# Sparse attention: one shift and one reciprocal for the four row tiles of a head, with waits for the whole head

## The reference, cut to what matters

```python
def attend_block(args):
    ...
    score = jnp.where(causal[None], score, -jnp.inf)
    _, idx = lax.top_k(score, topk)
    valid = idx <= t_pos[None, :, None]
    k_sel = gather(k, idx)
    v_sel = gather(v, idx)
    logits = jnp.einsum('bthd,btjd->bthj', q_b, k_sel).astype(jnp.float32) * ATTN_SCALE
    logits = jnp.where(valid[:, :, None, :], logits, -jnp.inf)
    probs = jax.nn.softmax(logits, axis=-1).astype(v.dtype)
    return jnp.einsum('bthj,btjd->bthd', probs, v_sel)
...
return (o * jax.nn.silu(z)) @ w_out
```

## Time and profile before

| | |
|---|---|
| median of 3 runs | 1798.1 us (1792.12 to 1801.71) |
| span of the profiled execution | 1793.1 us; its own time is not listed apart, and the median is 5.0 us above the span |
| TensorE busy | 1615.7 us (90%) |
| VectorE busy | 723.9 us (40%) |
| ScalarE busy | 520.4 us (29%) |
| GpSimd busy | 593.7 us (33%) |
| mean granted TensorE clock | 0.912 of full speed |
| masks, exponentials and scalings of the 16 heads | from 770.8 to 953.3 us of the span |

### The profile page before, as it was taken

The page is one execution under the profiler, slowest core; times in us unless marked ns, Lnnn a source line. Parts: engine busy times, 40 slices in busy tenths (PEclk is TensorE's granted clock), DMA queues, the critical chain, the costliest instruction groups (busy, mean ns, idle before and its releaser), DMA issues. The chain is left out here.

```text
span 1793.1 us, 23133 instructions
## 1 busy us (share of the span) xinstructions
PE 1615.7 (90%) x9729; PEld 1347.6 (75%) x9729; DVE 723.9 (40%) x1479; ACT 520.4 (29%) x842; POOL 593.7 (33%) x247
## 2 busy tenths in 40 slices
PE   6998999999989978988998989679999877959899
PEld 6896876999978755856667988677887643548889
DVE  4022430231252646967662161402301455587331
ACT  2443224332122232233442122432221234311211
POOL 5333421333332464426532433132442260500213
PEclk9998999999999988999999999889999776569769
DMA  4222310324223211311113222222332000000103
GB/s 148 92 71 71 94 47 1 95 95 177 71 71 107 79 63 47 94 48 47 42 43 133 80 94 88 98 66 75 94 95 71 1 1 1 0 30 1 63 20 102
DMA packets 116913, 121.58 MB, mean 68 GB/s; under 512 B 14799, under 2 KB 111033, under 8 KB 116554
## 3 DMA queue, kind: packets, MB, share of 16 engines
q1 hardware_dynamic: 109232, 111.90, 19.8%
q10 hardware_dynamic: 7578, 8.21, 1.4%
HBM read 113.80 MB, written 6.29 MB: 67 GB/s over the span
## 5 line engine op out<-in xcount | busy, mean ns | idle before, releaser
L175 POOL TENSOR_TENSOR w_low<-w_ring,w_high 128x2048 fp32r<-128x2048 f32 (+2 forms) x95 | 422.4, 4448 | 927.3 <-ACT w_high L166 927.2
L191 PE MATMUL ps<-w_high,xT_high 128*128 128x256 f32 (+1 forms) x1056 | 306.7, 290 | 32.7 <-ACT heads L1753 11.8
L191 PE MATMUL ps<-w_low,xT_high 128*128 128x256 f32 (+1 forms) x1056 | 301.6, 286 | 0.0
L191 PE MATMUL ps<-w_high,xT_low 128*128 128x256 f32 (+1 forms) x1056 | 301.5, 285 | 0.0
L166 ACT ACTIVATE w_high<-w_ring 128x2048 fp32r<-128x2048 f32 (+2 forms) x95 | 174.1, 1834 | 372.2 <-PE ps L191 359.5
L191 PE MATMUL ps<-xT_high,w_high 128*128 128x512 f32 (+3 forms) x624 | 255.0, 409 | 8.7 <-DVE mix_a L724 7.7
L191 PE MATMUL ps<-xT_low,w_high 128*128 128x512 f32 (+3 forms) x624 | 250.9, 402 | 0.0
L191 PE MATMUL ps<-xT_high,w_low 128*128 128x512 f32 (+3 forms) x624 | 250.6, 402 | 0.0
L191 PEld LDWEIGHTS ps<-w_high,xT_high 128*128 128x128 f32 x1056 | 205.7, 195 | 38.8 <-DVE xT_low L826 12.1
L191 PEld LDWEIGHTS ps<-w_low,xT_high 128*128 128x128 f32 x1056 | 205.6, 195 | 1.3 <-issue 1.2
L191 PEld LDWEIGHTS ps<-w_high,xT_low 128*128 128x128 f32 x1056 | 205.2, 194 | 0.0
(11 more groups left out here) (499 smaller groups left out, 2422.5 us busy)
## 6 DMA issues: line engine op xcount, KB each, us to landing
w_ring<-in_gla_w_in_dram SPq DMA_DIRECT2D x24, 1024.0 KB, 5.4
w_ring<-in_dsa_w_in_dram SPq DMA_DIRECT2D x19, 1024.0 KB, 5.2
w_ring<-in_w_in_dram SPq DMA_DIRECT2D x18, 1024.0 KB, 5.2
w_ring<-in_gla_w_out_dram SPq DMA_DIRECT2D x8, 1024.0 KB, 5.2
w_ring<-in_ple_gate_w_dram SPq DMA_DIRECT2D x8, 1024.0 KB, 5.0
w_ring<-in_dsa_w_out_dram SPq DMA_DIRECT2D x8, 1024.0 KB, 5.0
w_ring<-in_w_out_dram SPq DMA_DIRECT2D x8, 640.0 KB, 4.2
x_scratch<-x SPq DMA_DIRECT2D x4, 1024.0 KB, 6.8
```

The costliest lines, as they stand in the source:

```text
L175: self.nc.gpsimd.tensor_tensor(self.w_low[:, i % RING, 0:k, 0:cols], self.w_ring[:, n % RING, 0:k, 0:cols], self.w_high[:, i % RING, 0:k, ...
L191: return self.nc.tensor.matmul(out, lhs, rhs, start=first, stop=last, skip_group_check=not check)
```

## The change

The four shifts of a head become one operation on four columns behind the fourth mask, and the four reciprocals one operation behind the fourth exponential. ScalarE waits once a head, for that shift; VectorE waits for all four exponentials before the reciprocal, and for the reciprocal before the first scaling. The semaphores `peak_shift` and `inv_total` count heads instead of row tiles. Nothing else is changed.

```diff
@@ exps(h), ScalarE
-                        act.wait_ge(sem["peak_shift"], past["peak_shift"] + m + 1)
+                        if j == 0:
+                            act.wait_ge(sem["peak_shift"], past["peak_shift"] + h + 1)
@@ mask(h), VectorE
-                        dve.wait_ge(sem["masked"], past["masked"] + m + 1)
-                        nc.vector.tensor_scalar(shift[:, i:i + 1], peak[:, i:i + 1], -ATTN_SCALE, None, ALU.mult).then_inc(sem["peak_shift"], add("peak_shift", 1))
+                    heads = slice(h % 2 * NT, (h % 2 + 1) * NT)
+                    dve.wait_ge(sem["masked"], past["masked"] + NT * (h + 1))
+                    nc.vector.tensor_scalar(shift[:, heads], peak[:, heads], -ATTN_SCALE, None, ALU.mult).then_inc(sem["peak_shift"], add("peak_shift", 1))
@@ normalise(h), VectorE
+                    heads = slice(h % 2 * NT, (h % 2 + 1) * NT)
+                    dve.wait_ge(sem["exps"], past["exps"] + NT * (h + 1))
+                    nc.vector.reciprocal(inv[:, heads], total[:, heads]).then_inc(sem["inv_total"], add("inv_total", 1))
+                    dve.wait_ge(sem["inv_total"], past["inv_total"] + h + 1)
                     for j in range(NT):
                         m = NT * h + j
                         i = m % (2 * NT)
-                        dve.wait_ge(sem["exps"], past["exps"] + m + 1)
-                        nc.vector.reciprocal(inv[:, i:i + 1], total[:, i:i + 1]).then_inc(sem["inv_total"], add("inv_total", 1))
-                    for j in range(NT):
-                        m = NT * h + j
-                        i = m % (2 * NT)
-                        dve.wait_ge(sem["inv_total"], past["inv_total"] + m + 1)
                         row = prob[:, h % 2, j, 0:(j + 1) * P]
                         nc.vector.tensor_scalar(row, row, inv[:, i:i + 1], None, ALU.mult).then_inc(sem["prob_ready"], add("prob_ready", 1))
```

## The result

| | before | after |
|---|---|---|
| median, 4 runs each | 1795.1 us (1788.4 to 1801.7) | 1848.6 us (1842.4 to 1854.4) |
| ratio | | 1.0292 [1.0262, 1.0322] |
| span of the profiled execution | 1793.1 us | 1849.6 us (own time 1851.4) |
| TensorE, VectorE busy | 1615.7, 723.9 us | 1633.3, 741.9 us |
| mean granted TensorE clock | 0.912 | 0.904 |

The change makes the kernel 53 us slower, 2.9%. VectorE has six operations less in each head and is busy for 18 us more.

A forecast was written before the change was run, and what follows sets the result against it. TensorE was taken to bound iterations with a projection, with no slack in the chain through VectorE's copy of `probT`; the terms summed to 55.9 us on the 1798.1 median, giving 1854 us, range 1842 to 1866.

The forecast's parts named there:

- term 6: Iterations 12 and 13, already bound by the copy's chain: exponentials 1.5 us later, third scaling caught, 0.35; together 3.7 us.
- Terms 2 and 3: Head loop: `gT_high` 1.0 to 1.5 us later; third scaling falls 0.01 to 0.08 us behind `gT_low` instead of ahead.
- Rival A: Race lost only in part: third scaling still slips ahead in iterations up to 8; 24 us more, 1822; chance 0.13.
- Rival B: Third scaling always slips ahead, leaving only the exponentials' delay: 10.8 us more, 1809; chance 0.12.
- Term 4: Odd iterations 1 to 11: fourth scaling waits out `w_low`, copy 5.8 us later; 39.0 for five, 6.0 for the last.
- clock term: Odd iterations: TensorE's clock, lowered after the gap, adds 2.0 us each, taken between 1.56 and 2.9.
- Term 7: Iterations 2, 4 and 6: start 1.5 us later, two scalings caught instead of three; 0.1 us each, 0.3 more.
- Term 8: Before the loop: head 0's wide shift is held until `w_low` ends; 3.3 us more, bounds 0.4 and 4.1.
- Rivals C and D: C: delayed exponentials are covered, 1798, chance 0.06. D: VectorE's queue counts, 7.7 us less, 1790, chance 0.04.

The follow-up runs named there:

- The extra reciprocal: Kernel before, plus an unused one-column reciprocal ahead of each head's scalings: 1795.1 us, ratio 1.0000.
- the shifts alone: Kernel before with only the four-column shift and ScalarE's one wait a head, reciprocals as they were: 1808.2 us, ratio 1.0066.
- the kernel before with the wait: Kernel before, with GpSimd's `gT_low` waiting until the four scalings of the same iteration are done: 1777.7 us, ratio 0.9897.
- narrow shifts: Changed kernel, with head 0's shifts as four one-column operations again: 1847.5 us, ratio 1.0279 to the kernel before.
- reciprocals alone: Kernel before with only one reciprocal a head, which the first scaling waits for; shifts as they were: 1824.2 us, ratio 1.0155.

## Why the prediction was right

The sign, the mechanism and the size came out: 1854 forecast, 1848.6 measured; 55.9 us as a sum, 53.5 between the medians. In part that is luck: terms 4 and 7 came out lower than forecast (by 2.4 and 2.9 us), term 6 higher by 2.1, and 4.2 us of the span's difference lie outside all terms. By the terms, from the lengths of the iterations in the two traces:

| term | predicted | measured |
|---|---|---|
| iterations 1, 3, 5, 7, 9 | 39.0 | 7.9 + 6.8 + 7.7 + 6.7 + 8.1 = 37.2 |
| iteration 11 | 6.0 | 5.4 |
| iterations 8, 10 | 3.2 | 3.0 |
| iterations 12, 13 | 3.7 | 5.8 |
| iterations 2, 4, 6 | 0.3 | -2.6 |
| iteration 0 | 0.4 | 0.1 |
| before the loop | 3.3 | 3.5 |
| sum | 55.9 | 52.4 |

What is left of the span's difference, 4.2 us, lies in stages that the change doesn't touch; their length varies from run to run and isn't explained here.

- **Terms 2 and 3, the start and the race**: right. `gT_high` came at M+5.30 (5.27 predicted; its two summands, 3.05 and 2.18, give 5.23, and the 0.04 from shift to exponential wasn't named), the first scaling at M+5.64 (5.59), and the third scaling was caught in all iterations from 1 on, 0.045 to 0.12 us behind `gT_low` where 0.01 to 0.08 was predicted. The extra reciprocal shows how narrow the choice was on the other side: a third scaling that led by 0.03 passed, one that led by 0.004 (at 796.70, by the trace's finer digits) did not, though the scaling ahead of it was held too. Rival A, at 1822, fell by these margins. Rival B is the measured outcome of the shifts alone.
- **Term 4**: the two parts can be told apart. In the five odd iterations TensorE's busy time grew from 57.10 to 67.09 us in all, 2.0 each, for the same work at a granted 0.82 to 0.91, as the clock term of 2.0 had it (single ones 1.3 to 2.7). The rest, 27.2, is 5.45 each where the hold was put at 5.8. The step was sized with `gT_low` at 1.52 and `w_low` at 4.79 from the earlier trace rows; they lasted 1.35 and 4.61, together 0.35 less. Before, scalings had run beside the beginning of each, and these seem to have stretched the two rows: where GpSimd came behind all scalings, in the kernel before with the wait, they lasted 1.29 and 4.59.
- **Term 6** was too small by 2.1, for the clock, which it left out and had in its upper bound alone. Iteration 12, before and after:

```profile
936.00:945.23 9.23, 7.00 (x27) 4.44 (x27) 6.67 (x23) 3.91 (x11) 3.92 (x2) 0.87 0.34 114
...
981.65:993.44 11.79, 7.92 (x27) 4.95 (x27) 6.16 (x17) 3.46 (x11) 1.32 (x1) 0.79 0.19 65
```

It grew by 2.56 us: TensorE's busy time for the same products by 0.92, at a granted 0.79 for 0.87, and its idle time by 1.64, where 1.85 was predicted. From iteration 13 to the last product of the heads it was 3.2: 2.3 of busy time, at 0.73 for 0.83, and 0.9 idle. So the waits came out below the term, 2.6 for 3.7, and 3.2 of clock came on top.
- **Term 7** was wrong in sign. It counted the holds (a gap of 2.31 us on TensorE after, 2.17 before) and took the clock as unchanged. But the granted clock of iterations 2, 4 and 6 stayed at 1.00, where two of them had 0.89 before. A nearly equal gap went with either clock, also before (2.15 at 1.00 in iteration 6); what decides between them these runs don't show.
- **Term 8**: right, by 0.2. The wide shift was held to the end of `w_low` as the 128x4 cast of the load phase was the earlier trace rows, and with narrow shifts the hold was gone.
- **Rivals C and D**: nothing hid the delay. D's rule, to minimize the count of operations, is the Trainium skill's ("VectorE: DVE Perf Modes", "Rules for kernel authors"); here 96 operations less in 16 heads went with 53 us more. VectorE waited for ScalarE ahead of every reciprocal (1.77 us in iteration 9), so that fewer operations on it had nothing to shorten.

## What to carry to other kernels

When operations on an engine that doesn't bound are put together, count not what they cost but what they shift: here 0.12 us more between two VectorE operations decided which of two engines came first, and the loser stood for 4.7 us behind a long GpSimd operation. Look for such near-ties in the trace, and where one is found, order the long GpSimd work behind the short VectorE work with a wait of its own; that gained 18.5 us on the kernel before. A whole-group wait also moves everything behind it in the queue of the engine that waits, so follow that queue to each of its consumers.

## What the runs showed of the hardware that was not expected

- A shift of four columns is held by GpSimd and one of one column isn't: 3.76 against 0.15 us behind the same `w_low`, 0.59 to 0.81 behind a rotation. A reciprocal of four columns took 0.18 us in every reading here, also in the middle of a `w_low` (reciprocals alone, head 0).
- Who begins first decides within a few hundredths: a scaling that led by 0.02 or 0.03 us passed, one that came 0.02 behind was held. One that led by 0.004 was held as well, but the scaling ahead of it had been held too.
- In the kernel with one more reciprocal, where the first of four scalings led by 0.02, all four passed and GpSimd's `gT_low` was held for 2.38 us instead of some 1.3. In the kernel before, in iterations 2, 4 and 6, the first of four led by 0.08 and passed alone, and the next three were held; where the third led by 0.03 to 0.11, the fourth was held. So the number of scalings still to come doesn't decide it. What differs in the three iterations is the lead of 0.02 and the unused reciprocal ahead; which of them it is wasn't tried by itself.
- Stalls of 5.5 us on TensorE went with a granted clock of 0.82 to 0.91 for the iteration; stalls of 2.3 us left it at 1.00 in iterations 2, 4 and 6.
